# Latent attention with its exponentials and rotated halves in PSUM, and norms made on four token columns

## The chip, the cores and the metric

One core of a Trainium2 chip runs one program. The metric is the device time of one execution in microseconds (us). Engines are named as the profile names them: PE is TensorE (matrix products), PEld its weight loads, DVE VectorE, ACT ScalarE, POOL GpSimd, SP the engine that issues most of the DMAs. A core has 128 partitions; SBUF is the large on-chip memory, PSUM the one of eight banks of 512 fp32 columns into which PE writes.

## The reference

Four transformer layers over 512 tokens of 1024 features, fp32. The first two (windowed attention with sinks; block-sparse attention) end in an RMS norm, the "final norm". The last two modulate their input by a condition vector `c` and end in layer norms. The last one is latent attention, and it is the one that the change is mostly about:

```python
def mla_mixer(h, positions, w_in, q_norm_g, kv_norm_g, w_uq, w_uk, w_uv, w_out):
    proj = h @ w_in
    q_c, kv_c, k_r, z = jnp.split(proj, [MLA_Q_RANK, ...], axis=-1)   # 256, 128, 64, 2048 wide
    q_c, kv_c = rms_norm_2(q_c, q_norm_g), rms_norm_2(kv_c, kv_norm_g)
    q = jnp.einsum('bsr,rhd->bshd', q_c, w_uq)
    q_nope, q_rope = q[..., :MLA_NOPE], q[..., MLA_NOPE:]
    q_rope, k_rope = apply_rope(q_rope, ...), apply_rope(k_r, cos, sin)
    q_lat = jnp.einsum('bshd,rhd->bshr', q_nope, w_uk)
    ...
        s = jnp.einsum('bqhr,bkr->bhqk', ql, kv_c) + jnp.einsum('bqhd,bkd->bhqk', qr, k_rope)
        p = jax.nn.softmax(jnp.where(mask, s * ATTN_SCALE, -jnp.inf), axis=-1)
        o_lat = jnp.einsum('bhqk,bkr->bqhr', p, kv_c)
    ...
    o = jnp.einsum('bshr,rhd->bshd', o_lat, w_uv).reshape(B, S, MLA_WIDTH)
    return (o * jax.nn.silu(z)) @ w_out
# in the block around it
    x = layer_norm(DEEPNORM_ALPHA * x + (1.0 + gate[:, None, :]) * y, ln_g[l], ln_b[l])
```

## The kernel before

The kernel keeps activations transposed: features on the partitions, the 512 tokens along the columns. `hT` holds the residual stream as eight chunks of 128 features. Weights come in units of 128 x 1024. SP loads a unit into a ring of four (`raw`); ACT rounds it to its high part (`split_hi`, L531), POOL subtracts to get the low part (`split_lo`, L445), and PE makes every large product as three (`mm3`, L949 to L951: high by high, high by low, low by high). POOL does hardly anything else. Each engine has its own program, in the order in which it was written, and the engines wait for one another by semaphores that only count up.

**Norms.** A norm needs a sum over features, and features lie on partitions, so PE makes it: a product of the squares with `mean_w` (all entries 1/1024) puts the mean of each token, repeated on all 128 partitions, into a bank (`mean_square`, L979 for the final norm; L1335 for the latents). ACT takes the root of 128 x 512 values, DVE the reciprocal of 128 x 512 values (L1490, L1988, L1996), and the result, `rstd` or `rstd_q`, `rstd_kv`, multiplies the features. Behind the final norm DVE makes the modulated input (`modulate`, L1862 and L1857, with ACT's L766 between), for which PE waits with the next projection; then `residual` (L1871, eight instructions) and ACT's `residual_bias` (L773) turn `hT` into the residual term.

**Latents.** PE projects two query latents into banks 0 and 1, then the key/value latent into bank 2 and the rotary key into bank 3. In the fifth of the eight steps of each of the last two it makes the mean of the squares (banks 4 and 5). DVE multiplies the latents by gain and `rstd` (L1990, L1997) and makes the low parts (L1994); it rotates the key (L2002 to L2007). PE then makes the queries of the first two heads (`queries`), transposes the key/value latent (L1433), and goes on with `latent_queries`, which needs the low parts of the queries (`nope_lo`, L2012).

**Head loop.** Sixteen heads, in eight pairs. A pair has eight score blocks (m = 0 to 7; two heads by four blocks of 128 queries; block m has 128, 256, 384 or 512 keys), and two sets of buffers alternate. For a block PE makes the scores in a bank (`o_scores`, L1382 to L1385), DVE the maximum (L2028) and its scaled negative (L2030), ACT the exponential with its sum from the bank into SBUF tile `o_p` (L878), DVE the reciprocal of the sum (L2035) and the product `o_p` times it, in place (L2037), PE the transposes (`o_transpose`, L1393), ACT the copy into `o_pt` (L886), PE the latent output (`o_latent`, L1401). PE's order within a pair is: gate projection, scores 0 and 1, half of the second gate projection, and then for m = 2 to 10: transposes of m - 2, scores of m, latent output of m - 3, with quarters of the second gate projection at m = 5 and 9; then the next pair's queries, this pair's values, the next pair's latent queries. Meanwhile DVE rotates the next pair's queries (`rotate`, L2018, L2019, L2023), ACT and POOL split them (L863, L505). Ahead of the loop stand `residual(1)` on DVE and `residual_bias(1)` on ACT: the eight chunks of `hT` are multiplied by `rstd` and the gain column, then the bias is added. Only the sums behind the output projection need them.

## Time and profile before

| | us |
|---|---|
| median of 3 runs | 2105.71 (2102.74 to 2109.05) |
| the profiled execution, own time | 2105.03 |
| its span, first to last instruction | 2103.0 |
| PE busy | 1975.6 |
| DVE, ACT, POOL busy | 1016.6, 840.0, 805.9 |
| mean granted clock of PE | 0.971 |

The head loop runs from about 1690 to 1980 us of the span, the latents from 1644 to 1690, and the final norm at about 1280. The page's times are those of the profiled execution. A timeline row has the start, the duration (of several merged instructions, from the first start to the last end), the engine, the line and the operation with tiles and shape; in brackets the idle time of that engine before it and what ended it. In a row on groups, `x` is a count, followed by the busy time in us and the mean of one in ns. A granted clock of 1.00 is 2.4 GHz, one of 0.50 is 1.2 GHz; a value between them is a stretch in which it changed.

### The profile page before, as it was taken

What the parts mean: (1) busy time and instruction counts of PE and PEld (TensorE: products, weight loads), DVE (VectorE), ACT (ScalarE), POOL (GpSimd) and SP (SyncE); (2) the same over time, 40 slices, a digit from 0 to 9 for tenths busy, and PEclk for the clock granted to TensorE, in tenths of its full rate; (3) what the DMA queues carried; (4) which work ended last, traced back from release to release, by engine and by line L of the source; (5) the groups of instructions that cost most, each with busy time, mean ns of one, the idle gap of its engine ahead of it and who ended that gap; (6) DMA issues with size and microseconds to landing.
All of it is one profiled execution on the core that took longest, in us unless ns stands there. A gap on an engine that the chain in (4) does not pass through costs nothing.

```text
span 2103.0 us, 29110 instructions
## 1 busy us (share of the span) xinstructions
PE 1975.6 (94%) x9640; PEld 1638.0 (78%) x9640; DVE 1016.6 (48%) x2286; ACT 840.0 (40%) x1520; POOL 805.9 (38%) x382
## 2 busy tenths in 40 slices
PE   7999999999988999999999997999999789999896
PEld 5897888888777889878888886777887567777684
DVE  5555665211636666356553116658113655555414
ACT  4564222233444666342222325222222465555432
POOL 3533544444363100135444443445443332232340
PEclk9999999999999989999999999999999999999998
DMA  7532544222242112135442322323232111121121
GB/s 240 159 103 101 195 166 167 93 97 100 71 150 66 47 46 76 36 114 190 160 159 100 100 92 72 107 91 105 90 100 80 60 53 59 50 70 40 61 80 40
DMA packets 70026, 209.55 MB, mean 100 GB/s; under 512 B 9739, under 2 KB 15115, under 8 KB 69948
## 3 DMA queue, kind: packets, MB, share of 16 engines
q1 hardware_dynamic: 57724, 174.72, 25.2%
q10 hardware_dynamic: 12224, 33.85, 5.0%
q8 instruction: 41, 0.67, 0.1%
q14 instruction: 37, 0.30, 0.0%
HBM read 196.90 MB, written 8.49 MB: 98 GB/s over the span
## 4 chain that ended last, share of the span: by engine, by line
PE 58%; issue 21%; POOL 9%; DVE 8%; ACT 4%; POOLq 0%; DVEq 0%; ACTq 0%
PE bank L949 14%; PE bank L951 14%; PE bank L950 14%; POOL wsp L445 9%; PE bank L1227 3%; PE bank L1382 2%; DVE gen L2037 2%; PE bank L1200 1%; PE bank L1401 1%; PE bank L1211 1%; PE bank L1095 1%; PE bank L1393 1%; ACT wsp L531 1%; PE bank L1072 1%; PE bank L1223 1%
## 5 line engine op out<-in xcount | busy, mean ns | idle before, releaser
L445 POOL TENSOR_TENSOR wsp<-raw,wsp 128x1024 fp32r<-128x1024 f32 x294 | 730.5, 2491 | 1051.4 <-ACT wsp L531 1051.3
L949 PE MATMUL bank<-xs,wsp 128*128 128x512 f32 x1320 | 522.1, 396 | 19.5 <-issue 8.4
L950 PE MATMUL bank<-xs,wsp 128*128 128x512 f32 x1320 | 516.1, 391 | 0.0
L951 PE MATMUL bank<-xs,wsp 128*128 128x512 f32 x1320 | 516.1, 391 | 0.0
L531 ACT ACTIVATE wsp<-raw 128x1024 fp32r<-128x1024 f32 x294 | 306.9, 1052 | 229.9 <-PE bank L951 199.9
L949 PEld LDWEIGHTS bank<-xs,wsp 128*128 128x128 f32 x1320 | 249.4, 189 | 76.8 <-issue 15.3
L949 PE MATMUL bank<-xk,wsp 128*128 128x512 f32 x752 | 295.3, 393 | 9.4 <-DVE xk L1503 5.1
L950 PE MATMUL bank<-xk,wsp 128*128 128x512 f32 x752 | 294.2, 391 | 0.0
L951 PE MATMUL bank<-xk,wsp 128*128 128x512 f32 x752 | 294.2, 391 | 0.0
L951 PEld LDWEIGHTS bank<-xs,wsp 128*128 128x128 f32 x1320 | 249.2, 189 | 52.5
L950 PEld LDWEIGHTS bank<-xs,wsp 128*128 128x128 f32 x1320 | 249.6, 189 | 52.0 <-issue 1.4
L1503 DVE TENSOR_TENSOR xk<-mid,xk 128x512 fp32r<-128x512 f32 x86 | 61.1, 710 | 382.4 <-ACT xk L571 382.4
L571 ACT ACTIVATE xk<-mid 128x512 fp32r (+1 forms) x86 | 54.3, 631 | 331.2 <-PE bank L951 331.2
L949 PEld LDWEIGHTS bank<-xk,wsp 128*128 128x128 f32 x752 | 142.2, 189 | 41.6 <-DVE xk L1503 6.3
L951 PEld LDWEIGHTS bank<-xk,wsp 128*128 128x128 f32 x752 | 142.2, 189 | 29.8
L950 PEld LDWEIGHTS bank<-xk,wsp 128*128 128x128 f32 x752 | 142.3, 189 | 29.3
L1553 DVE CUSTOM_DVE_ANT_0 gen<-gen 128x1024 f32<-128x1024 f32 x48 | 124.7, 2598 | 14.0 <-issue 14.0
L587 ACT ACTIVATE tmp<-tmp 128x512 f32<-128x512 f32 x44 | 27.8, 632 | 245.4 <-DVE tmp L1541 245.4
L1543 DVE TENSOR_TENSOR mid<-bank,rstd 128x512 f32 (+1 forms) x44 | 30.4, 691 | 155.4 <-PE bank L951 155.4
L1227 PE MATMUL bank<-mid 128*128 128x64 f32 x640 | 90.1, 293 | 0.0
L734 ACT ACTIVATE mid<-mid,stat 128x128 f32<-128x128 f32 (+3 forms) x128 | 70.8, 554 | 38.6 <-DVE stat L1805 38.1
L1227 PEld LDWEIGHTS bank<-mid 128*128 128x128 f32 x640 | 84.7, 209 | 0.0
(286 smaller groups left out, 2504.2 us busy)
## 6 DMA issues: line engine op xcount, KB each, us to landing
raw<-weights SPq DMA_DIRECT2D x294, 512.0 KB, 3.5
gen<-ada ACTq DMA_DIRECT2D x48, 512.0 KB, 3.5
tmp<-mid SPq DMA_DIRECT2D x64, 128.0 KB, 3.0
bias_b<-bias_row ACTq DMA_DIRECT2D x1, 4096.0 KB, 38.1
mid<-bias_b SPq DMA_DIRECT2D x8, 512.0 KB, 3.9
hT<-xT SPq DMA_DIRECT2D x2, 1024.0 KB, 10.1
bias_a<-bias_row ACTq DMA_DIRECT2D x1, 2048.0 KB, 18.0
mid<-bias_a SPq DMA_DIRECT2D x8, 256.0 KB, 2.9
```

The costliest lines, as they stand in the source:

```text
L445: pool.tensor_tensor(wsp[:, slot, 1, :], raw[:, slot, :], wsp[:, slot, 0, :].bitcast(F32), ALU.subtract).then_inc(w_ready, 1)
L531: act.activation(wsp[:, u % RING, 0, :], raw[:, u % RING, :], ACT.Copy).then_inc(hi_done, 1)
L571: act.activation(xk[:, k % 2, 0, :], mid[:, i * RING + k, :], ACT.Copy).then_inc(xk_hi, 1)
L734: act.activation(b_s[b][:, r, 0:w], b_s[b][:, r, 0:w], ACT.Exp, scale=-1.0, bias=stat[:, b, r:r + 1], accum_out=stat[:, b, 4 + r:5 + r]).t ...
L949: pe.matmul(dst, w[0], x[0], start=first, stop=False)
L950: pe.matmul(dst, w[0], x[1], start=False, stop=False)
L951: return pe.matmul(dst, w[1], x[0], start=False, stop=last)
L1227: x = pe.matmul(dst[:, (1 + r) * HD:(2 + r) * HD], b_pt[b][:, r, kb * P:kb * P + P], vtok[:, r, kb * P + pp * HD:kb * P + pp * HD + HD], s ...
L1382: pe.matmul(dst[:, 0:w], ql[e][:, q], kvn[:, 0:w], start=True, stop=False)
L1503: dve.tensor_tensor(xk[:, k % 2, 1, :], mid[:, i * RING + k, :], xk[:, k % 2, 0, :].bitcast(F32), ALU.subtract).then_inc(xk_ready, 1)
L1553: dve.tensor_tensor_reduce(out=ada_st[k], in0=ada_st[k], in1=cond, scale=1.0, scalar=0.0, op0=ALU.mult, op1=ALU.add, accum_out=mod_sum[:, ...
L2037: dve.tensor_scalar(o_p[b][:, 0:w], o_p[b][:, 0:w], stat[:, b, 3:4], None, ALU.mult).then_inc(o_prob, 1)
```

## The change

In the head loop the exponential stays in the score bank, and DVE's product reads the bank and writes `o_p`. Since the bank is then read until the product is done, the scores of block m wait for the product of m - 2 (`o_prob`) and not for its exponential. ACT no longer waits for the transposes of m - 2; DVE's product does. The second rotation product is written into its own bank and the sums take one input from there; the rotated key is built in bank 7.

The residual of the last layer leaves DVE. POOL multiplies one chunk by `rstd` in each turn of its loop, behind the first weight split, and one behind the loop; ACT applies gain and bias to a chunk at the end of each pair.

In the final norm and at the latents PE writes the means of the four blocks of 128 tokens as four columns, one value for a token on its partition (`columns`); ACT and DVE work on 128 x 4 values, and PE spreads the result over the partitions again by four products with `ident` (`spread`), into the bank from which DVE reads it. The latents are multiplied by their gain before the norm is known; the normalised query latents stay in banks 0 and 1. The second half of the value projection waits until the residual has read bank 7.

```diff
+            def residual(j):
+
+                pool.tensor_tensor(hT[:, j, :], hT[:, j, :], rstd[:, :], ALU.mult).then_inc(mod_x, 1)
+
             with pool.Fori(0, PAIRS - 1) as hp:
                 for k in range(RING):
                     u = O_H + 5 + k
                     split_lo(u % RING, hp * RING + u)
+                    if k == 0:
+                        residual(hp)
                     if k == 2:
                         rope_lo(hp + 1)
+            residual(PAIRS - 1)
...
             def o_exp_of(m, r, hp):
 
                 b, w = m % 2, P * (m % 4 + 1)
-                if m >= 2:
-                    act.wait_ge(o_t, hp * 8 + (8 * r + m - 1))
+                scores = bank[SCORE_BANKS[r][b]][:, 0:w]
                 act.wait_ge(o_nm, hp * 8 + (8 * r + m + 1))
-                act.activation(o_p[b][:, 0:w], bank[SCORE_BANKS[r][b]][:, 0:w], ACT.Exp, scale=QK_SCALE,
-                               bias=stat[:, b, 1:2], accum_out=stat[:, b, 2:3]).then_inc(o_exp, 1)
+                act.activation(scores, scores, ACT.Exp, scale=QK_SCALE, bias=stat[:, b, 1:2],
+                               accum_out=stat[:, b, 2:3]).then_inc(o_exp, 1)
...
+                j = hp + r
+                act.wait_ge(mod_x, j + (16 + DC + 1))
+                act.activation(hT[:, j, :], hT[:, j, :], ACT.Identity, scale=modg[:, 1, bass.ds(j + 16, 1)],
+                               bias=modg[:, 1, bass.ds(j + 24, 1)]).then_inc(alpha_done, 1)
...
-            residual_bias(1)
...
+                if n == NORM_FINAL:
+                    act.activation(std_col[:, :], bank[7][:, 0:NB], ACT.Sqrt, bias=eps[:, 0:1]).then_inc(std_ready, 1)
+                    return
...
+            def columns(dst, src, first, last):
+
+                for blk in range(NB):
+                    x = pe.matmul(dst[:, blk:blk + 1], src[:, blk * P:blk * P + P], mean_w[:, 0:1],
+                                  start=first and blk == 0, stop=last and blk == NB - 1)
+                return x
+
+            def spread(dst, done, count):
+
+                pe.wait_ge(done, count)
+                for blk in range(NB):
+                    x = pe.matmul(dst[:, blk * P:blk * P + P], rstd_col[:, blk:blk + 1].to_broadcast([P, P]), ident[:, :],
+                                  start=True, stop=True)
+                return x
...
+                if n == NORM_FINAL:
+                    pe.wait_ge(sq_used, 8 * n + DC - 1)
+                    columns(bank[7], rstd, True, True).then_inc(sq_used, 1)
+                    spread(bank[7], rstd_ready, n + 1).then_inc(rstd_ready, 1)
+                    return
...
             for n in range(2):
+                if n:
+                    pe.wait_ge(mod_x, 2 * DC)
                 for q in range(4):
...
                 for k in range(DC):
-                    if k == 4:
+                    if k == 3:
                         pe.wait_ge(c_sq, 3 if n else 2)
                         for j in squared:
-                            x = pe.matmul(bank[at][:, :], mean_w[:, :], tmp[:, j, :], start=j == squared[0],
-                                          stop=j == squared[-1])
+                            x = columns(bank[at], tmp[:, j, :], j == squared[0], j == squared[-1])
                         x.then_inc(c_mean, 1)
+                    if k == 6:
+                        spread(bank[at], c_std, 5 if n else 2).then_inc(c_std, 1)
...
                 if m >= 2:
-                    pe.wait_ge(o_exp, hp * 8 + (8 * r + m - 1))
+                    pe.wait_ge(o_prob, hp * 8 + (8 * r + m - 1))
...
-                dve.tensor_tensor(tmp[:, 1, :], bank[3][:, :], sinb, ALU.mult).then_inc(r_part, 1)
+                dve.tensor_tensor(bank[3][:, :], bank[3][:, :], sinb, ALU.mult).then_inc(r_part, 1)
...
-                dve.tensor_scalar(o_p[b][:, 0:w], o_p[b][:, 0:w], stat[:, b, 3:4], None, ALU.mult).then_inc(o_prob, 1)
+                if m >= 2:
+                    dve.wait_ge(o_t, hp * 8 + (8 * r + m - 1))
+                dve.tensor_scalar(o_p[b][:, 0:w], bank[SCORE_BANKS[r][b]][:, 0:w], stat[:, b, 3:4], None, ALU.mult
+                                  ).then_inc(o_prob, 1)
...
             rotate(0, 0)
-            residual(1)
```

How the instructions stand on the engines is shown at three places, before and then with the change. An order row has the line, the operation, its tiles and shape, and the semaphores that it waits for.

VectorE in the head loop, the first block of a pair and the start of the second, before:

```order
L2028 TENSOR_REDUCE stat<-bank 128x1 [waits o_qk]
L2030 TENSOR_SCALAR stat<-stat 128x1 [waits o_max]
L2035 RECIPROCAL stat<-stat 128x1 [waits o_exp]
L2037 TENSOR_SCALAR gen<-gen,stat 128x128 [waits o_rec]
L2027 REGISTER_ALU
L2028 TENSOR_REDUCE stat<-bank 128x1 [waits o_qk]
L2030 TENSOR_SCALAR stat<-stat 128x1 [waits o_max]
```

and with the change:

```order
L2077 TENSOR_REDUCE stat<-bank 128x1 [waits o_qk]
L2079 TENSOR_SCALAR stat<-stat 128x1 [waits o_max]
L2084 RECIPROCAL stat<-stat 128x1 [waits o_exp]
L2088 TENSOR_SCALAR gen<-bank,stat 128x128 [waits o_rec]
L2076 REGISTER_ALU
L2077 TENSOR_REDUCE stat<-bank 128x1 [waits o_qk]
L2079 TENSOR_SCALAR stat<-stat 128x1 [waits o_max]
```

The order is the same; the product now takes its input from a bank, where it took it from `gen` (the tile `o_p`).

ScalarE from the end of one pair (splits of units for the next) into the first blocks of the next, before:

```order
L530 REGISTER_ALU [waits raw_in1]
L531 ACTIVATE wsp<-raw 128x1024 [waits unit_used]
L531 ACTIVATE wsp<-raw 128x1024 [waits unit_used,raw_in2]
L877 REGISTER_ALU
L878 ACT_TABLE_LOAD
L878 ACTIVATE gen,stat<-bank,stat 128x128 [waits o_nm]
L530 REGISTER_ALU [waits raw_in3]
L531 ACTIVATE wsp<-raw 128x1024 [waits unit_used]
```

and with the change:

```order
L538 REGISTER_ALU [waits raw_in1]
L539 ACTIVATE wsp<-raw 128x1024 [waits unit_used]
L930 REGISTER_ALU
L931 ISA [waits mod_x]
L931 ISA
L931 ACTIVATE hT<-hT,modg 128x512
L539 ACTIVATE wsp<-raw 128x1024 [waits unit_used,raw_in2]
L888 REGISTER_ALU
L889 ACT_TABLE_LOAD
L889 ACTIVATE bank,stat<-bank,stat 128x128 [waits o_nm]
L538 REGISTER_ALU [waits raw_in3]
L539 ACTIVATE wsp<-raw 128x1024 [waits unit_used]
```

The residual of one chunk has come between the two weight splits, ahead of the table load and the first exponential.

VectorE between the modulated input of the last layer and the first queries (`mid` and `gen` hold the latents, `gsp` the low parts), before:

```order
L1988 RECIPROCAL mid<-stdb 128x512 [waits c_std]
L1990 SCALAR_TENSOR_TENSOR mid<-bank,colp,mid 128x512 [waits vec_step]
L1990 SCALAR_TENSOR_TENSOR mid<-bank,colp,mid 128x512
L1994 TENSOR_TENSOR gsp<-mid,gsp 128x512 [waits qc_hi] x2
L1996 RECIPROCAL tmp<-mid 128x512 [waits c_std]
L1997 SCALAR_TENSOR_TENSOR gen<-bank,colp,tmp 128x512 [waits vec_step]
L2002 TENSOR_TENSOR tmp<-bank,gen 64x512 [waits unit_used,trig_ready]
L2003 TENSOR_TENSOR tmp<-bank,gen 64x512 [waits vec_step]
L2005 TENSOR_TENSOR tmp<-tmp 64x512 [waits kr_ready]
L2007 TENSOR_TENSOR gen_r<-tmp,gen_r 64x512 [waits kr_ready]
```

and with the change:

```order
L2031 TENSOR_SCALAR mid<-bank,colp 128x512 [waits c_sq]
L2031 TENSOR_SCALAR mid<-bank,colp 128x512 [waits vec_step]
L2033 RECIPROCAL rstd_col<-std_col 128x4 [waits c_std,vec_step]
L2036 TENSOR_TENSOR bank<-mid,bank 128x512 [waits c_std]
L2036 TENSOR_TENSOR bank<-mid,bank 128x512
L2039 TENSOR_TENSOR gsp<-bank,gsp 128x512 [waits qc_hi] x2
L2042 TENSOR_SCALAR gen<-bank,colp 128x512 [waits c_sq]
L2044 RECIPROCAL rstd_col<-std_col 128x4 [waits c_std,vec_step]
L2046 TENSOR_TENSOR gen<-gen,bank 128x512 [waits c_std]
L2051 TENSOR_TENSOR tmp<-bank,gen 64x512 [waits unit_used,trig_ready]
L2052 TENSOR_TENSOR bank<-bank,gen 64x512 [waits vec_step]
L2054 TENSOR_TENSOR bank<-tmp,bank 64x512 [waits kr_ready]
```

The gain products stand ahead of the reciprocals, these have 4 columns where they had 512, and the products with the spread norm (`bank` as second input) follow them.

## Rows read from the trace of the kernel before

**Rows 1.** The page: busy time of each engine.

```profile
PE 1975.6 (94%) x9640; PEld 1638.0 (78%) x9640; DVE 1016.6 (48%) x2286; ACT 840.0 (40%) x1520; POOL 805.9 (38%) x382
```

**Rows 2.** Waits of PE in the head loop: total us, times, longest.

```profile
PE bank L1393 <- DVE gen L2037: 22.7, 11, 5.7
```

**Rows 3.** Timeline of PE in one pair: start, us, instruction, idle time before.

```profile
1729.39 0.38 PE L1382 MATMUL bank<-gen 128*128 128x128 f32 x2
...
1735.72 0.33 PE L1393 MATMUL bank<-ident,gen 128*128 128x128 f32 x1 [2.31 <-DVE gen L2037]
...
1753.43 0.47 PE L949 MATMUL bank<-gsp,wsp 128*128 128x512 f32 x1
```

**Rows 4.** Windows of PE: length, busy (instructions), clock, DMA share, GB/s.

```profile
1736.50:1737.00 0.50, 0.50 (x3) 0.69 0.50 98
...
1740.00:1740.50 0.50, 0.50 (x4) 0.90 0.00 0
```

**Rows 5.** Timeline of DVE in the same pair.

```profile
1731.27 4.39 DVE L2037 TENSOR_SCALAR gen<-gen,stat 128x128 f32<-128x128 f32 x1
...
1737.29 0.55 DVE L2028 TENSOR_REDUCE stat<-bank 128x1 f32<-128x384 f32 x1
...
1738.77 0.16 DVE L2035 RECIPROCAL stat<-stat 128x1 f32<-128x1 f32 x1 [0.74 <-ACT gen L878]
1738.97 0.42 DVE L2037 TENSOR_SCALAR gen<-gen,stat 128x384 f32<-128x384 f32 x1
```

**Rows 6.** Timeline of POOL there.

```profile
1728.57 7.01 POOL L445 TENSOR_TENSOR wsp<-raw,wsp 128x1024 fp32r<-128x1024 f32 x3
```

**Rows 7.** Timeline of ACT there, and a group of ACT lines: xcount, busy us, mean ns.

```profile
1730.58 0.37 ACT L878 ACTIVATE gen<-bank,stat 128x128 f32<-128x128 f32 x1
...
L773 ACT ACTIVATE hT<-hT,modg 128x512 f32<-128x512 f32 x4 | 2.7, 723 | 0.0
```

**Rows 8.** Timelines of DVE and POOL in the first pair.

```profile
1697.01 0.41 DVE L2028 TENSOR_REDUCE stat<-bank 128x1 f32<-128x256 f32 x1
...
1698.44 1.02 DVE L2037 TENSOR_SCALAR gen<-gen,stat 128x256 f32<-128x256 f32 x1
...
1694.66 4.65 POOL L445 TENSOR_TENSOR wsp<-raw,wsp 128x1024 fp32r<-128x1024 f32 x2 [7.06 <-ACT wsp L531]
```

**Rows 9.** Groups of DVE lines, forms apart: xcount, busy us, mean ns.

```profile
L1827 DVE TENSOR_SCALAR gen<-bank,stat 128x64 f32<-128x64 f32 x64 | 18.1, 283 | 45.1 <-PE bank L1227 33.9 <-PE bank L1238 10.6
...
L2037 DVE TENSOR_SCALAR gen<-gen,stat 128x512 f32<-128x512 f32 x16 | 7.8, 487 | 0.6
...
L1946 DVE TENSOR_SCALAR mid<-bank,colp 128x512 f32<-128x512 f32 x8 | 6.1, 805 | 9.3 <-PE bank L951 9.3
```

**Rows 10.** Timelines of PE and DVE at the first pair.

```profile
1697.14 0.47 PE L1393 MATMUL bank<-ident,gen 128*128 128x128 f32 x1 [5.74 <-DVE gen L2037]
...
1683.96 7.50 DVE L1871 SCALAR_TENSOR_TENSOR hT<-hT,modg,rstd 128x512 f32<-128x512 f32 x8
```

**Rows 11.** Timelines of PE and DVE at the latents.

```profile
1659.47 1.88 PE L1335 MATMUL bank<-tmp,mean_w 128*128 128x512 f32 x4
...
1680.46 0.47 PE L949 MATMUL bank<-gsp,wsp 128*128 128x512 f32 x1 [3.57 <-DVE gsp L2012]
...
1669.23 3.34 DVE L1996 RECIPROCAL tmp<-mid 128x512 f32<-128x512 f32 x1
```

**Rows 12.** Timelines of PE and DVE at the final norm.

```profile
1289.89 0.76 PE L949 MATMUL bank<-wsp,xs 128*128 128x512 f32 x1 [6.58 <-DVE xs L1857]
...
1284.07 3.35 DVE L1490 RECIPROCAL rstd<-stdb 128x512 f32<-128x512 f32 x1 [2.23 <-ACT stdb L558]
```

**Rows 13.** Timeline of PE in the second attention: products with few columns.

```profile
652.24 1.00 PE L1168 MATMUL bank<-gen 128*128 128x14 f32 x8
```

**Rows 14.** Windows of PE in the second attention, columns as in rows 4.

```profile
722.00:723.00 1.00, 0.19 (x2) 1.00 0.71 217
...
744.00:745.00 1.00, 1.00 (x7) 0.50 0.00 0
```

## What I expect of the time

> **What bounds the kernel now.** I read the page first, then the waits of TensorE in the head loop, then one pair of heads on every engine, then the two stretches in which norms are made. The page says that TensorE is busy for 94% of the span [rows 1]. So an edit counts only where TensorE stands still, or where it runs at its lower clock because it stood still. In the head loop almost all its standing still has one cause: it waits for VectorE's normalised probabilities, L2037: 22.7 us, of which the first pair has 5.74, seven pairs 2.31 each, and three short waits the rest [rows 2, 3, 10]. One of the seven shows the pattern: the scores of the first block start at 1729.39, TensorE does what it can, stands for 2.31 us, and goes on at 1735.72 with the first transpose [rows 3]. Behind that gap the granted clock falls to the lower level (1.2 GHz) at 1736.7 and is back at 2.4 GHz at 1740.1: the half microseconds in which it changes show 0.69 and 0.90 [rows 4]. Why is VectorE late? Its multiplication of 128 columns took 4.39 us [rows 5], though it started at 1731.27, early enough. GpSimd was in three weight splits back to back, from 1728.57 to 1735.58 [rows 6], and VectorE's instruction ended at 1735.66, 0.08 us after the last of them. That is the cause I take. The same rows hold the control: in the first pair, while GpSimd worked from 1694.66 to 1699.31, VectorE's maximum over 256 columns of PSUM took 0.41, but its multiplication of 256 columns, from SBUF to SBUF, took 1.02 [rows 8], where even 512 columns take 0.487 on average over the loop [rows 9]. So the SBUF-to-SBUF multiplication is held by GpSimd, and the instruction that reads PSUM isn't.
>
> **The pair of heads, parts removed.** With the exponentials left in PSUM the multiplication reads PSUM, and by the control it isn't held. The 2.31 us of standing go. With them goes the lower clock: 3.4 us, in which half the work is done, so 1.7 us. Together 4.0 us of the 24.0 that lie between 1729.39 and 1753.43 [rows 3, 4].
>
> **The pair of heads, parts added.** First, the multiplication is slower in itself. From SBUF, 512 columns took 0.487 [rows 9]. From PSUM, with one column as scalar, 64 columns took 0.283, and 512 columns with two such scalars 0.805 [rows 9]; that leaves about 1.04 ns for a column, so 0.75 for 512, 0.62 for 384, 0.48 for 256 and 0.35 for 128, which is 0.27 to 0.07 more than before, 0.67 for four blocks. Second, ScalarE gets a residual instruction of 0.72 to 0.8 us (the one with columns as scalars stands in [rows 7]) at the end of a pair, directly ahead of the next pair's first exponential, and ScalarE is tight there: that exponential began at 1730.58, and its row names no idle time before it. It moves to about 1731.4. Maximum to finished product then ends near 1732.5, and TensorE asks for it at 1733.4: 0.8 us of slack, so it is hidden. Third, the later blocks. From a block's maximum to its product there pass 2.1 us before (1737.29 to 1739.39 for 384 columns, [rows 5]) and 2.3 with the slower product. For the third block TensorE has only some 1.8 us of other work meanwhile, since the second block's product is now also late: a wait of 0.5 to 0.75. For the fourth, seventh and eighth blocks VectorE's own chain of maximum and product runs behind by 0.1, 0.3 and 0.45. That makes 1.5, of which about 0.3 was there before among short gaps: I take 1.2 net, with 0 (the chain catches up) and 2.4 (each of eight blocks waits 0.3) as bounds. The transposes already stood ahead of the scores in TensorE's order, so that scores now wait for the product and not for the exponential adds no wait. Nor does ScalarE's dropped wait give anything. A pair gains 4.0 - 1.2 = 2.8, and seven pairs 19.6.
>
> **The first pair.** The residual (eight instructions on VectorE, 7.50 us, [rows 10]) no longer stands ahead of the first maximum, so the 5.74 us of standing [rows 10] go, and the lower clock behind them costs at least the same 1.7. Less 1.2 that is 6.3. GpSimd does the residual's product in its loop now: half of a weight split of 2.34 us [rows 6], 1.2 us a pair. Behind it on GpSimd stand the splits of units that are first needed a pair later, so 20 us of slack hide it, and without that cover it would cost 1.2 a pair. ScalarE's wait for it comes 30 us later. The residual of all chunks is needed only by the output projection's sums after the loop.
>
> **Latents.** From 1659.47, where the mean square starts, to 1680.46, where the first latent queries start after 3.57 us of standing [rows 11], there pass 21.0 us. TensorE's own work there is 14.0 without the means (60 products of 0.226 us, the pace of the stretches that do not wait, and four transposes). VectorE's 3.35 us reciprocals [rows 11, 12] and its multiplication and sums held by GpSimd made the standing. They shrink to four columns, or take one input from PSUM; counted forward, the low halves of the queries are ready just as TensorE has finished the kvn transposes, so the 3.57 go. But TensorE's means cost more: three full products (six instructions, 2.6 us, four of them at 0.43 each in the first, [rows 11]) become twelve one-column products and eight spreading ones. Each is two instructions, and instructions with 14 columns came 0.11 apart [rows 13], no cheaper than with 128, since a weight load goes with each. 40 x 0.11 = 4.4. So 14.0 + 4.4 + 0.2 of start-up = 18.6, a gain of 2.4. Bounds: 0.5 (a wait of 2 is left) and 3.6.
>
> **Final norm.** TensorE stood for 6.58 us [rows 12] behind a chain in which the reciprocal has 3.35 [rows 12]. It becomes one of four columns, 0.2 (128 x 1 took 0.16, [rows 5]), and the root loses 0.35 (0.72 against 0.37 for 512 and 128 columns, [rows 7]). That is 3.5 less. The spread adds eight instructions at 0.11, 0.9, or 1.8 at the lower clock: 2.2 of gain, bounds 1.2 and 3. The new wait of the second half of the value projection, for bank 7, finds the residual long done.
>
> **The sum** against the profiled execution's own time, 2105.03 (span 2103.0; the median of the three runs is 2105.71): 19.6 + 6.3 + 2.4 + 2.2 = 30.5, so 2074.5.
>
> **The rivals.**
> 1. *The clock still falls in every pair.* The new short waits sit in the stretch of small products, and these might not hold the clock. The gain of 1.7 is lost eight times: 2074.5 + 13.6 = 2088. Against it: in the attention before, a microsecond with a busy share of only 0.19 left the clock at its upper level [rows 14]. 0.13.
> 2. *The waits in the pair vanish.* If ScalarE's exponential gets shorter when it writes PSUM, the chain of 2.3 us shrinks to TensorE's 1.8. Then 8 x 1.2 = 9.6 more: 2065. No row has ScalarE writing to PSUM. The Trainium skill, page "PSUM — Partial Sum Buffer", section "Specifications (TRN2)", says that ScalarE writes PSUM faster than SBUF; no run here shows it. 0.12.
> 3. *ScalarE becomes the bound at a pair's start.* If the residual with its offsets from registers takes 1.6 instead of 0.8, the slack is gone, and up to 0.8 comes in each pair: 2081. 0.06.
> 4. *The change doesn't do what it says:* VectorE is held whatever it reads while GpSimd works. Then the 19.6 and most of the 2.4 stay away, and 6.3 + 2.2 are left: 2097. Against it stands the control in [rows 8]. The Trainium skill, page "SBUF — State Buffer", section "Who interferes with whom", has the rule: GpSimd shares a pair of ports with VectorE, held for a whole instruction, and only a VectorE instruction in a two-port mode or with two SBUF inputs needs it. By that rule, the trace agrees: 0.41 against 1.02. 0.03.
> 5. *Slower: the lower clock stays through the small products.* In the attention before, a stretch ran at half clock while TensorE was fully busy, with 7 instructions in a microsecond [rows 14] against 9 at 0.11 apart. If a wait early in a pair starts such a stretch and it lasts through the 14 us of small products, each pair loses 3 (7 against 9) to 7 (half); with 5 that is 8 x 5 = 40: 2114. It decides from 3.8 us of loss in a pair. 0.04.
>
> **How the numbers follow.** My forecast has 0.62; with its bounds it spans 2067 to 2082. The range 2062 to 2089 takes in rivals 1 to 3 and leaves out 4, 5 and the tails, some 0.1 to 0.15. What can be told from no change is 0.3%, 6.3 us. Faster by more: all but rival 5 and a sliver, 0.95; within: 0.01; slower: 0.04.
>
> **What would show it.** In the pairs: no wait of TensorE for the first product over 0.3 us, a clock of 1.00 throughout, and a multiplication of 128 columns at 0.35 beside GpSimd's splits; and 21.2 us from the first scores to the end of the first head pair's products, where 24.0 stood. At the latents: TensorE's wait for the low halves under 0.5, forty instructions on one-column and spreading products. At the final norm: some 4.4 us of standing in all in place of 6.58. I am wrong if products from PSUM are still stretched while GpSimd works, if a half-clock stretch is left in each pair, or if ScalarE's first exponential starts later than 2.8 us after the first scores.

## The result, and the profile after

The changed kernel takes 2069.03 us (median of 4 runs, 2067.32 to 2070.8) against 2105.3 of the kernel before: a ratio of 0.983 (95% interval 0.981 to 0.984), 36.3 us less where I had forecast 30.5 less. The profiled execution took 2069.23 us, its span is 2067.4 (2103.0 before), so the two traces differ by 35.6.

The page of the changed kernel, busy time of each engine, beside [rows 1]:

```profile
PE 1963.5 (95%) x9688; PEld 1637.3 (79%) x9688; DVE 969.7 (47%) x2281; ACT 839.3 (41%) x1520; POOL 813.4 (39%) x390
```

PE has 48 instructions more and is all the same busy 12 us less: the time that it no longer spends at its lower clock outweighs them. The waits of PE between 1683 and 1955 us, beside [rows 2] (line waited at, what for, total us, times, longest):

```profile
PE bank L1430 <- DVE gen L2088: 8.0, 16, 0.7
PE bank L963 <- DVE xk L2093: 2.5, 1, 2.5
```

22.7 us have become 8.0, in sixteen pieces, two in each pair. The third pair in the timeline of PE, beside [rows 3]: its first scores, its first, third and last transposes:

```profile
1752.55 0.38 PE L1419 MATMUL bank<-gen 128*128 128x128 f32 x2
...
1756.42 0.27 PE L1430 MATMUL bank<-ident,gen 128*128 128x128 f32 x1
...
1760.09 0.55 PE L1430 MATMUL bank<-ident,gen 128*128 128x128 f32 x3 [0.63 <-DVE gen L2088]
...
1771.00 0.66 PE L1430 MATMUL bank<-ident,gen 128*128 128x128 f32 x4 [0.36 <-DVE gen L2088]
```

The first transpose no longer waits; the third block's does, for 0.63, and the eighth's, for 0.36. From one pair's first scores to the next there pass 34.5 us, each of the seven times, where 42.0 passed in the first pair and 37.6 to 37.8 in the others. Why the first transpose doesn't wait is in the timelines of DVE, POOL and ACT at the same place, beside [rows 5 to 7]:

```profile
1755.12 0.35 DVE L2088 TENSOR_SCALAR gen<-bank,stat 128x128 f32<-128x128 f32 x1
...
1759.42 0.62 DVE L2088 TENSOR_SCALAR gen<-bank,stat 128x384 f32<-128x384 f32 x1
```

```profile
1754.62 2.39 POOL L446 TENSOR_TENSOR wsp<-raw,wsp 128x1024 fp32r<-128x1024 f32 x1 [0.55 <-ACT wsp L539]
1756.97 1.28 POOL L515 TENSOR_TENSOR hT<-hT,rstd 128x512 f32 x1
```

```profile
1751.37 0.80 ACT L931 ACTIVATE hT<-hT,modg  x1
...
1754.45 0.32 ACT L889 ACTIVATE bank<-bank,stat 128x128 f32<-128x128 f32 x1
```

The product of 128 columns takes 0.35 us in the middle of a weight split (4.39 before). ACT's residual of 0.80 stands ahead of the first exponential, which starts 1.90 us after the first scores (1.19 before, [rows 3, 7]); the product is done at 1755.47 and PE asks for it at 1756.42. The clock holds through the wait that is left, in half a microsecond without any work (windows of PE: length, busy time and instructions, clock, DMA share, GB/s), beside [rows 4]:

```profile
1759.50:1760.00 0.50, 0.00 (x0) 1.00 0.82 336
1760.00:1760.50 0.50, 0.41 (x4) 1.00 0.09 33
```

The groups by line with shapes apart (count, busy us, mean ns; then idle time before), beside [rows 9]:

```profile
L2088 DVE TENSOR_SCALAR gen<-bank,stat 128x512 f32<-128x512 f32 x16 | 12.0, 751 | 0.6
L2088 DVE TENSOR_SCALAR gen<-bank,stat 128x128 f32<-128x128 f32 x16 | 5.6, 351 | 0.8 <-DVE stat L2084 0.3
L889 ACT ACTIVATE bank<-bank,stat 128x128 f32<-128x128 f32 x16 | 5.4, 340 | 9.3 <-DVE stat L2079 9.3
```

At the final norm, PE (beside [rows 12]): four columns of means, four spreading products, the first value product.

```profile
1280.51 1.02 PE L990 MATMUL bank<-mean_w,rstd 128*128 128x1 f32 x8 [2.27 <-DVE rstd L1510]
1282.10 2.07 PE L998 MATMUL bank<-ident,rstd_col 128*128 128x128 f32 x8 [0.57 <-DVE rstd_col L1528]
...
1286.64 0.77 PE L963 MATMUL bank<-wsp,xs 128*128 128x512 f32 x1 [2.47 <-DVE xs L1898]
```

From the means to the first value product there pass 6.1 us where 7.9 passed. At the latents (beside [rows 11]) nothing waits any more between the means and the latent queries:

```profile
1657.03 1.84 PE L990 MATMUL bank<-mean_w,tmp 128*128 128x1 f32 x16
...
1660.91 1.05 PE L998 MATMUL bank<-ident,rstd_col 128*128 128x128 f32 x8
...
1676.33 0.48 PE L963 MATMUL bank<-gsp,wsp 128*128 128x512 f32 x1
```

**Where the 35.6 us come from.** I laid the two traces of PE beside one another by instructions that stand in both, and read how far the changed kernel is ahead:

| stretch | ahead at its end | gained in it |
|---|---|---|
| start to the final norm (the change leaves it alone) | 1.5 | 1.5 |
| final norm, until the clock is back | 2.5 | 1.0 |
| rest of the third layer (not touched) | 2.2 | -0.2 |
| latent projections to the first scores | 3.8 | 1.6 |
| head loop | 33.3 | 29.5 |
| output projection (not touched) | 35.6 | 2.3 |

The head loop's 29.5 splits into standing and clock. Standing: 22.7 - 8.0 = 14.7. Clock: before, PE was at work at the lower clock for 5.4 us in the first pair, 3.2 in the second and 3.4 in each of six more, 29.1 in all, of which half is lost: 14.5. After, the loop has no such stretch. 14.7 + 14.5 = 29.2.

### The profile page after: what moved, and what is told of

The parts are those of the page before. It is cut to its first block, busy times and chain, and to the rows that moved or that the text cites. A ratio compares the mean times of both kernels' runs of the same rounds, so it can differ in the third digit from the quotient of the medians.

```text
span 2067.4 us, 29274 instructions
## 1 busy us (share of the span) xinstructions
PE 1963.5 (95%) x9688; PEld 1637.3 (79%) x9688; DVE 969.7 (47%) x2281; ACT 839.3 (41%) x1520; POOL 813.4 (39%) x390
## 4 chain that ended last, share of the span: by engine, by line
PE 62%; issue 21%; POOL 9%; DVE 6%; ACT 2%; POOLq 0%; DVEq 0%; ACTq 0%
PE bank L963 16%; PE bank L965 15%; PE bank L964 15%; POOL wsp L446 9%; PE bank L1261 3%; PE bank L1234 1%; PE bank L1245 1%; PE bank L1419 1%; PE bank L1129 1%; PE bank L1438 1%; PE bank L1017 1%; PE bank L1106 1%; PE bank L1257 1%; PE bank L1430 1%; PE bank L1117 1%
## 5 line engine op out<-in xcount | busy, mean ns | idle before, releaser
L965 PEld LDWEIGHTS bank<-xk,wsp 128*128 128x128 f32 x752 | 141.7, 188 | 29.5
```

Of the source, the lines that this page charges most:

```text
L965: return pe.matmul(dst, w[1], x[0], start=False, stop=last)
```

## The experiments

All ran on the same chips as runs of the kernel before, whose median was 2103.8 to 2105.5 us.

| run | what it is | median us | ratio to before (95%) |
|---|---|---|---|
| e1_exp_psum | before, exponentials in PSUM | 2076.35 | 0.987 (0.985 to 0.988) |
| e2_pool_late | before, GpSimd's splits held back | 2078.14 | 0.988 (0.986 to 0.989) |
| e3_residual | before, residual moved | 2106.75 | 1.001 (1.000 to 1.002) |
| e4_exp_sbuf | changed, exponentials back in SBUF | 2101.29 | 0.998 (0.998 to 0.999) |
| e5_norms | before, norms on columns | 2101.29 | 0.998 (0.997 to 0.999) |
| e6_forms | changed, one VectorE instruction more a pair | 2080.35 (one run) | |
| v1_late_sbuf | changed, SBUF and splits held back | 2065.21 | 0.981 (0.980 to 0.982) |
| v2_gate | changed, gate projection cut otherwise | 2067.1 | 0.982 (0.980 to 0.983) |
| v3_filler | changed, fillers at the final norm | 2066.48 | 0.981 (0.980 to 0.983) |
| v4_all | v1, v2 and v3 together | 2060.97 | 0.979 (0.978 to 0.981) |
| r_after | changed, again | 2068.4 | 0.983 (0.982 to 0.984) |

### Is it the exponentials' place? (e1_exp_psum)

```diff
-                if m >= 2:
-                    act.wait_ge(o_t, hp * 8 + (8 * r + m - 1))
+                scores = bank[SCORE_BANKS[r][b]][:, 0:w]
                 act.wait_ge(o_nm, hp * 8 + (8 * r + m + 1))
-                act.activation(o_p[b][:, 0:w], bank[SCORE_BANKS[r][b]][:, 0:w], ACT.Exp, scale=QK_SCALE,
-                               bias=stat[:, b, 1:2], accum_out=stat[:, b, 2:3]).then_inc(o_exp, 1)
+                act.activation(scores, scores, ACT.Exp, scale=QK_SCALE, bias=stat[:, b, 1:2],
+                               accum_out=stat[:, b, 2:3]).then_inc(o_exp, 1)
...
-                    pe.wait_ge(o_exp, hp * 8 + (8 * r + m - 1))
+                    pe.wait_ge(o_prob, hp * 8 + (8 * r + m - 1))
...
-                dve.tensor_scalar(o_p[b][:, 0:w], o_p[b][:, 0:w], stat[:, b, 3:4], None, ALU.mult).then_inc(o_prob, 1)
+                if m >= 2:
+                    dve.wait_ge(o_t, hp * 8 + (8 * r + m - 1))
+                dve.tensor_scalar(o_p[b][:, 0:w], bank[SCORE_BANKS[r][b]][:, 0:w], stat[:, b, 3:4], None, ALU.mult
+                                  ).then_inc(o_prob, 1)
```

> The kernel before, with one part of the change alone: exponentials stay in the score bank, VectorE's product reads the bank. My theory (VectorE's SBUF-to-SBUF product is held while GpSimd works, its product from PSUM isn't; the standing drags the clock down): pairs 2 to 8 take 34.5 us each in place of 37.7, so 22 us less. In the first pair the residual still stands ahead on VectorE: the wait of 5.74 us shrinks to about 2, so 4 less, and the clock there is uncertain by 2.7. Sum: about 2079 us (2075 to 2082). Rival, the gain comes from the residual that moved or from the norms: within 5 us of 2105.

Measured 2076.35: this part alone gains 28.3 us, where the whole change gains 36.3. Pairs take 34.5 us. In the first pair the wait is 1.66 (timeline of PE), and no lower clock follows it, nor is there one anywhere in this run's loop: the first pair takes 36.7.

```profile
1694.14 0.33 PE L1392 MATMUL bank<-ident,gen 128*128 128x128 f32 x1 [1.66 <-DVE gen L2038]
```

The pairs have the length of the changed kernel's, so the residual that the change puts on ScalarE and GpSimd costs them nothing. Ahead of the loop, though, this trace has a half-clock stretch that neither the kernel before nor the changed one has, from 1677.5 to 1684.3 (window of PE):

```profile
1680.00:1680.50 0.50, 0.50 (x3) 0.50 0.00 0
```

PE is at work for 5.2 us of it, so some 2.6 are lost. It starts in the standing for the latent queries, which the kernel before has at the same length (3.57 us, [rows 11]) without a fall. On the other hand the clock stays up at the output projection, where it fell before, which gives 2.3. The two nearly cancel: from the first scores of the loop to the output projection this trace gains 27.4 us, where the changed kernel gains 29.5.

### Is GpSimd the cause? (e2_pool_late)

```diff
                     u = O_H + 5 + k
+                    if k == 0:
+                        pool.wait_ge(o_prob, hp * 8 + 8)
                     split_lo(u % RING, hp * RING + u)
```

> The kernel before, exponentials still in SBUF; one wait is added: in each turn of its loop GpSimd begins its first weight split only when the eighth product of the pair is done, so that no split runs beside the products. My theory (GpSimd holds the product of 128 columns): no product over 0.5 us, TensorE's wait of 2.31 us and the half-clock stretch behind it are gone although nothing moves to PSUM; a pair takes 33.5 to 34.0 us, 7 x 3.9 = 27 less, and 4 less in the first pair: about 2074 us (2070 to 2079). Rival, the source in PSUM matters by itself or the scheduling of ScalarE does: no gain, 2105 us, and slower (over 2110) if TensorE now waits for the late splits.

Measured 2078.14, and pairs of 34.0 us. GpSimd splits one unit ahead of the products, stands until the eighth product is done, and then splits two (timelines of POOL and DVE, second pair, whose first scores start at 1724.83):

```profile
1724.00 2.37 POOL L445 TENSOR_TENSOR wsp<-raw,wsp 128x1024 fp32r<-128x1024 f32 x1
1742.92 4.72 POOL L445 TENSOR_TENSOR wsp<-raw,wsp 128x1024 fp32r<-128x1024 f32 x2 [16.54 <-DVE gen L2039]
```

```profile
1726.71 0.29 DVE L2039 TENSOR_SCALAR gen<-gen,stat 128x128 f32<-128x128 f32 x1
```

The same instruction, SBUF to SBUF, takes 0.29 where it took 4.39 [rows 5]. In the second to seventh pairs the wait and the lower clock are gone without anything in PSUM; the first keeps 1.60 us of waiting (1.66 in e1). The last pair, for which I hadn't placed a wait, still has its 2.31 us and a half-clock stretch behind it. That settles the cause, and it shows a second remedy whose pairs are 0.5 us shorter than the change's. The total is no lower than e1's all the same: the last pair keeps its wait, and the clock falls at the output projection, where it didn't in e1.

### The residual alone (e3_residual)

```diff
+                    if k == 0:
+                        residual(hp)
...
-            residual_bias(1)
...
-            residual(1)
```

> The kernel before, with one part alone: the residual goes to GpSimd's loop and to the end of ScalarE's pair. By my theory this is a loss by itself: GpSimd's product of 1.28 us stands in the run of splits that holds VectorE's first product, so the hold, TensorE's wait and the pair grow by 1.3 us, from 37.7 to 39.0, seven times 9 us more; in the first pair the wait of 5.74 becomes 2.31 + 1.3 = 3.6, 2 less. Sum: about 2112 us (2106 to 2114). Rival, the residual costs nothing wherever it stands and the first pair gains 5.74 and its clock: 2098 us.

Measured 2106.75, 2 us slower than before: the sign is right and the size isn't. The profiled execution is the fastest of the ten (2101.05; the slowest took 2108.79), so its trace shows the pattern but not the 2 us; what differs in the slower ones wasn't profiled. In five of seven later pairs the first product is held to the end of a run of splits that is now longer (DVE and POOL, second pair), and PE waits 3.5 us:

```profile
1723.83 4.91 DVE L2047 TENSOR_SCALAR gen<-gen,stat 128x128 f32<-128x128 f32 x1
```

```profile
1720.42 4.72 POOL L445 TENSOR_TENSOR wsp<-raw,wsp 128x1024 fp32r<-128x1024 f32 x2
1725.11 1.25 POOL L514 TENSOR_TENSOR hT<-hT,rstd 128x512 f32 x1
1726.33 2.33 POOL L445 TENSOR_TENSOR wsp<-raw,wsp 128x1024 fp32r<-128x1024 f32 x1
```

In the two others (the third and the fifth pair) GpSimd had paused for 0.54 us right before the split in which VectorE's product arrives, and the hold broke up: 1.98 us at the first product and 2.24 at the second (third pair):

```profile
1762.62 1.98 DVE L2047 TENSOR_SCALAR gen<-gen,stat 128x128 f32<-128x128 f32 x1
...
1765.96 2.24 DVE L2047 TENSOR_SCALAR gen<-gen,stat 128x256 f32<-128x256 f32 x1
```

I had counted one pattern for all. And the first pair gave 6.2 where I expected 2: there the first product took 1.60 us, and GpSimd had paused for 1.10 before the split. The kernel before has the same in its first pair, behind a pause of 7.06 [rows 8] (DVE):

```profile
1695.16 1.93 DVE L2037 TENSOR_SCALAR gen<-gen,stat 128x128 f32<-128x128 f32 x1
```

It ended at 1697.09, between the two splits of the run, the first of which ended at 1697.01. In the traces of all the runs the SBUF-to-SBUF instructions of 128 columns that met GpSimd in the loop fall into two groups. Eight came in the first instruction of a run, behind a pause of at least 0.53 us (one in the kernel before, one in e5, three each in e3 and e4), and ended 0.1 us after that instruction. 27 came in a later instruction of a run (the kernel before, e2 to e6) and ended 0.1 to 0.15 us after the last. What stays open is why.

### The exponentials taken back (e4_exp_sbuf)

The first diff of this section, turned round, on the changed kernel.

> The changed kernel with its exponentials back in SBUF, all else as changed. My theory: VectorE's first product is held again, and 1.3 us longer than in the kernel before, for GpSimd's residual product lies in the run of splits: pairs of 39.0 us in place of 34.5, 8 x 4.5 = 36 more, about 2104 us (2098 to 2108). Rival, the hold costs what it did before (3.2 a pair): 2095. Rival, the exponentials' place isn't what gained: under 2080.

Measured 2101.29, 32 us more than the changed kernel; pairs of 38.0 to 40.0 us, but the first 35.0. The two kinds of hold are those of the run before. So without the exponentials in PSUM all else that the change does is worth 3.4 us against the runs beside it (2104.68).

### The norms alone (e5_norms)

The changed kernel's norms, columns and rotation on the kernel before, with the exponentials and the residual as they were.

> The kernel before with the column norms (final norm and latents) and the rotation in PSUM alone; exponentials in SBUF, residual on VectorE ahead of the loop. From the two stretches of the changed kernel I now read 1.0 us at the final norm, where part of the standing removed lay in a half-clock stretch that stays, and 2.1 at the latents: about 2101.5 us (2099 to 2104), and pairs of 37.7 us as before. Rival, the terms as forecast, 2.2 and 2.4: 2100. Rival, the norms carry the 5 us by which the changed kernel beat my forecast: 2096.

Measured 2101.29: 4.2 us less than before, nearest to the 2101.5 of my new reading; 2100 can't be told from it, 2096 can. Pairs take 37.6 as before, the first 41.2, 0.8 less.

### Which instructions are held (e6_forms)

```diff
+                if not tail and r == 0:
+                    dve.tensor_scalar(s, a, 2.0, None, ALU.mult)
+                elif not tail:
+                    dve.tensor_tensor(d, a, s, ALU.mult)
+                elif r == 0:
+                    dve.tensor_tensor(d, a, c, ALU.mult)
+                else:
+                    dve.tensor_scalar(d, a, 2.0, None, ALU.mult)
```

(`a`, `c` and `d` are 128 columns of an SBUF tile that is free there, `s` 128 columns of the score bank.)

> The changed kernel with one VectorE instruction more in each pair, ahead of the first product, while GpSimd is in a weight split; 128 columns, its output used by nothing. In pairs 1, 3, 5 a product by a constant from SBUF to the score bank; in pairs 2, 4, 6 a product of an SBUF tile and the bank, to SBUF; in pair 7 a product of two SBUF tiles, to SBUF; in pair 8 a product by a constant from SBUF to SBUF. If what GpSimd holds is the form with all its data in SBUF, the first two take about 0.3 to 0.4 us and the last two end with GpSimd's run, several us. Rival, the output's place doesn't matter and an SBUF input is enough: the first is held too. Rival, only the form with one SBUF input and one SBUF output (pair 8) is held: pair 7 takes 0.35.

The groups of DVE lines with shapes apart:

```profile
L2089 DVE TENSOR_TENSOR stdb<-stdb 128x128 f32<-128x128 f32 x1 | 5.1, 5141 | 0.0
L2091 DVE TENSOR_SCALAR stdb<-stdb 128x128 f32<-128x128 f32 x1 | 5.1, 5066 | 0.0
L2085 DVE TENSOR_SCALAR bank<-stdb 128x128 f32<-128x128 f32 x3 | 0.8, 274 | 0.0
L2087 DVE TENSOR_TENSOR stdb<-stdb,bank 128x128 f32<-128x128 f32 x3 | 0.8, 268 | 0.0
```

Four forms with 128 columns, at the same place of a pair, each begun inside a GpSimd instruction: 5.1 us where all data lie in SBUF, 0.27 where one operand, be it the output, lies in PSUM. One bank in the instruction is enough. The pairs with the two short forms still take 34.5 us; in the pair with the first long one PE waits 3.9 us.

All data in SBUF isn't enough for a hold, though. The instructions on one column lie in SBUF too (`stat` to `stat`), and they are never held; eight and nine of them began and ended inside an instruction of GpSimd in the kernel before and took no longer than the others (its groups of DVE lines in the head loop):

```profile
L2030 DVE TENSOR_SCALAR stat<-stat 128x1 f32<-128x1 f32 x64 | 9.8, 154 | 2.2
L2035 DVE RECIPROCAL stat<-stat 128x1 f32<-128x1 f32 x64 | 10.5, 164 | 47.8 <-ACT gen L878 47.8
```

From how many columns on a product is held, no run shows. The Trainium skill, page "SBUF — State Buffer", section "Who interferes with whom", says that VectorE contends with GpSimd in a two-port mode or with two SBUF inputs, and that the loser is then blocked for the whole of the other's instruction. The trace agrees for two SBUF inputs (5.14) and for one SBUF input beside a bank (0.27); that the form with one SBUF input and SBUF output (5.07) ran in such a mode, the trace doesn't show. And the page speaks of one instruction of GpSimd, where here the hold went on over three of them, 5.1 us in all.

### The remedy that keeps SBUF (v1_late_sbuf)

The changed kernel with e4's edit, and e2's wait ahead of the split of k = 0, and once more behind the loop:

```diff
             residual(PAIRS - 1)
+            pool.wait_ge(o_prob, 8 * PAIRS)
```

> The changed kernel with exponentials back in SBUF and GpSimd's splits held until the eighth product of each pair (the last pair too). If the hold by GpSimd is the whole cause and the product from SBUF is 0.07 to 0.27 us shorter, pairs take 34.0 us in place of 34.5: 8 x 0.45 = 3.6 less than the changed kernel, about 2065.5 us (2063 to 2069). Rival, the later splits make TensorE or ScalarE wait at a pair's end: over 2071.

Measured 2065.21. Pairs of 34.0 us. PE's waits for the products in the loop:

```profile
PE bank L1434 <- DVE gen L2090: 4.3, 10, 0.6
```

GpSimd's idle time in a pair pays for it; VectorE's product is the cheaper one from SBUF (0.35 for 256 columns, 0.48 from PSUM). The median is 3.2 to 3.8 us below the changed kernel's two medians, with intervals that overlap; the 0.5 us of each pair are read from the traces.

### The waits that are left (v2_gate)

```diff
-                project(u0 + 1, z[1][:, :], hp, part=range(4))
+                project(u0 + 1, z[1][:, :], hp, part=range(3))
                 for m in range(2, 11):
+                    if m == 4:
+                        project(u0 + 1, z[1][:, :], hp, part=range(3, 4))
```

> The changed kernel with TensorE's second gate projection cut otherwise: three of its eight steps ahead of the first transposes where four stood, and the fourth ahead of the third block's transposes, where 0.63 us of waiting is left in each pair. If that wait and the 0.35 later come from VectorE's chain of maximum and product, the chain now starts 0.4 us earlier and the fourth step fills the rest: about 0.5 us less in each pair, 2065 us (2063 to 2068). Rival, the wait only moves to the second or fourth block: 2069.

Measured 2067.1, no more than 2 us below the changed kernel's two medians, with intervals that overlap; the traces show it: pairs of 34.23 us, 0.25 less, half of what I expected. The 0.63 before the third block's transposes has become 0.36 before the second's, and the 0.35 before the eighth's has stayed:

```profile
PE bank L1430 <- DVE gen L2090: 5.4, 15, 0.4
```

So the wait partly moved, as the rival had it; the last one doesn't come from the chain's early start.

### The clock at the final norm (v3_filler)

```diff
+                    filler(6)
                     pe.wait_ge(sq_used, 8 * n + DC - 1)
                     columns(bank[7], rstd, True, True).then_inc(sq_used, 1)
+                    filler(2)
                     spread(bank[7], rstd_ready, n + 1).then_inc(rstd_ready, 1)
+                    filler(10)
```

(`filler(n)` makes n products of `ident` and `mean_w` into bank 0, which nothing reads.)

> The changed kernel with 18 small products more on TensorE, of no use but to keep it at work, in its three gaps at the final norm (6, 2 and 10, about 0.22 us each). If the half-clock stretch there comes from the standing, it goes: the spread, the wait and the first value products run at full clock, 3 to 3.5 us less: 2066 us. Rival, the clock falls all the same: the fillers then take 0.43 us each, the last ten 4.3 us in a gap of 2.5, and it is 2 to 3 us slower: 2071.5.

Measured 2066.48, 2 to 2.5 us less than the changed kernel's two medians; the intervals overlap, so the stretch itself must show it. In the changed kernel the clock falls at 1281.5 and is back at 1291.7, and 7.2 us of PE's work lie in between (windows of PE):

```profile
1281.50:1282.00 0.50, 0.03 (x1) 0.50 0.00 0
...
1291.50:1292.00 0.50, 0.50 (x3) 0.78 0.00 0
```

With the fillers it never falls there; the spread takes 1.16 in place of 2.07 (window and timeline of PE):

```profile
1282.00:1282.50 0.50, 0.50 (x7) 1.00 0.00 0
```

```profile
1283.27 1.16 PE L998 MATMUL bank<-ident,rstd_col 128*128 128x128 f32 x8
1284.27 2.40 PE L1009 MATMUL bank<-mean_w,ident 128*128 128x128 f32 x20
1286.90 0.47 PE L963 MATMUL bank<-wsp,xs 128*128 128x512 f32 x1 [0.24 <-DVE xs L1904]
```

v4, which has the same fillers, has no fall there either, and the eleven traces without fillers all have one, so this is not chance: the standing is the cause of the lower clock here, and work without use prevents it. By the traces it saves 1.0 us before the first value product (7.4 us after the last product of the layer ahead, where 8.4 passed) and 2.5 behind it, half of the 5.1 us that ran at the lower clock there.

### All together (v4_all)

The edits of v1, v2 and v3 in one kernel.

> All that paid, in one kernel: exponentials in SBUF with GpSimd's splits held back, the other cut of the second gate projection, and the small products at the final norm. If the parts add: 2065.2 less 2.5 for the fillers and 1 to 2 for the gate projection (0.43 us of waiting are left in a pair): about 2061.5 us (2059 to 2064). Rival, they overlap or the clock gives it back elsewhere: 2064 to 2067.

Measured 2060.97, the fastest here, 0.979 of the kernel before (0.978 to 0.981), 7.4 to 8.1 us below the changed kernel's two medians. The parts add up. PE's waits for the products in the loop:

```profile
PE bank L1440 <- DVE gen L2098: 1.7, 9, 0.3
```

Pairs take 33.8 us.

### The changed kernel again (r_after)

> The changed kernel again, beside the two others. Median 2069.0 as before (2067 to 2071). The pairs take 34.5 us each again. Whether the half-clock stretches behind the value projection's wait (1.2 us, at 1358) and at the output projection's start (2.5 us of standing) come is not fixed by the program by my theory: one of them may be there now, 1.7 to 2.7 us each. Rival, the change removed them for good: none of them in this run either.

Measured 2068.4; pairs of 34.5. Neither of the two half-clock stretches came, so this run goes with the rival. The other traces say more. Behind the value projection the clock fell in all four kernels with the old final norm (before, e1, e2, e3), and of the nine traces with the new one only in v3. In turn, ahead of the last layer (at 1626 us in the changed kernel) it fell in eight of those nine, all but v3, and in none with the old norm. So it goes with the form of the norm: the new one moved a half-clock stretch from one place to another, 1.4 us gained and 1.6 lost. My theory that chance puts it there was wrong for this place. Why v3 goes with the old ones, and v4, which has the same fillers, with the new, stays open. At the start of the output projection, which is the same in all and where PE stands for 2.5 us and again for 1.5, it fell in e2, e3, e4, e5, e6, v2, v4 and the kernel before, and stayed up in e1, v1, v3 and both runs of the changed kernel; no part of the change goes with that. A window of PE there, first of the kernel before, then of the changed one:

```profile
1983.00:1983.50 0.50, 0.50 (x3) 0.50 0.00 0
```

```profile
1949.50:1950.00 0.50, 0.50 (x4) 1.00 0.00 0
```

The same standing is followed by a fall in one kernel and not in the next. So it is with the 3.6 us of standing at the old form of the latents: the clock fell in e1 and e2 and stayed up in e3 and the kernel before. What decides it the runs don't show, so the 2.3 us gained there aren't safely the change's.

## Why the prediction was right, and where it was off

- **What bounds, and why VectorE is late: right.** e1 and e4 show that the place of the exponentials carries 28 to 32 us; e2 takes GpSimd away and has the effect with nothing moved; e6 shows the form that is held, in four variants. The control in [rows 8] was weaker than I took it to be: it set a maximum that reads PSUM beside a multiplication in SBUF, two things that differ. Only e1 and e6 part the place from the operation.
- **Parts removed in a pair, 4.0 us: right.** In each of the seven pairs behind the first, the standing of 2.31 and the 1.7 of lower clock went: no stretch at half clock is left in any of the eight pairs, which rival 1 (2088) would have had. Rivals 4 (held anyway) and 5 (half clock through the small products) fell with it.
- **Parts added in a pair, 1.2 net: somewhat too much.** The product's own cost was right to the hundredth (0.351, 0.484, 0.618, 0.751 us for 128 to 512 columns, against 0.35, 0.48, 0.62, 0.75 worked out). The third block waits 0.63 (0.5 to 0.75 forecast) and the eighth 0.35 (0.45), but those that I gave the fourth and seventh, 0.4 together, aren't there. Part of the reason is that ScalarE's exponential is shorter into PSUM, 0.340 against 0.365 on average for 128 columns (one of them in [rows 7]) and 0.662 against 0.688 for 512, 0.025 each: rival 2 in kind, but not enough to remove the waits. A pair gained 3.1 to 3.2 where I had 2.8: 22.0 for seven against 19.6.
- **ScalarE's slack at a pair's start: right.** The residual took 0.80; the product was ready 0.95 us before PE asked (0.8 forecast). GpSimd's residual took 1.28 (1.2) and delayed nobody. What I hadn't seen is that this part, made alone, is a loss (e3): it is free only because the products no longer mind GpSimd.
- **The first pair, 6.3: too small, 7.5.** I took 1.7 for the clock as "at least"; by the windows of before, PE was at work for 5.4 us at the lower clock there, 2.7 lost. 5.74 + 2.7 - 1.0 of new waits is 7.4.
- **Latents, 2.4: right in mechanism and nearly in size.** From the first latent projection to the latent queries 34.7 us pass where 36.6 passed, and in the changed kernel 1.0 us more of that work fell at the lower clock, 0.5 lost: 1.9 + 0.5 = 2.4. 0.3 was given back before the first scores, so 1.6 is what arrived.
- **Final norm, 2.2: wrong in size, 1.0.** The standing shrank by 3.5, as worked out (2.27 + 6.58 to 2.27 + 0.57 + 2.47), and the spread cost 2.1 at the lower clock (the forecast had 0.9, or 1.8 at the lower clock, and took 1.3). The step that failed is that I priced the remaining standing removed at its full length. The clock had already fallen, and it came back 5.1 us after the first value product (3.1 before): the earlier start was spent on work at half speed. A gain that falls into a half-clock stretch counts about half. v3 shows the rest: with the clock kept up, about 2.5 us more arrive. The sign that I named, 4.4 us of standing, was also at odds with my own term: 6.58 less 3.5 is 3.1, and 3.04 came (0.57 + 2.47).
- **What I didn't forecast:** 2.3 us at the output projection, where the clock fell before and didn't after, and 1.3 net ahead of the final norm and behind it. Of the latter, the part ahead of the norm is run-to-run: in eleven traces with the same program up to the final norm, its means start anywhere from 1278.7 to 1282.0 us.

So the 5.1 us between forecast and trace are 3.5 in stretches that the change leaves alone, and 3.6 more in the loop (2.4 in seven pairs, 1.2 in the first), less 2.0 at the norms. The 3.5 are luck as far as the runs show, and without them the forecast is off by 1.6.

## What to carry to other kernels

When a VectorE instruction is long for its size, look at what GpSimd does in the same microseconds: a multiplication of 128 columns or more with all its data in SBUF can be held over a whole run of GpSimd's, and either one operand in PSUM or another time for GpSimd's work frees it; the second costs nothing on VectorE, and here it was the better one, by 0.5 us a pair. Count a wait that disappears together with the lower clock behind it, but price a start that moves earlier inside a half-clock stretch at half. Where PE must stand for several microseconds and the next work is dense, a few idle products can be worth more than the norm made cheaper.

## What the runs showed of the hardware that I had not expected

- The hold reaches over several instructions of GpSimd: 5.14 and 5.07 us for 128 columns, over three instructions and to within 0.2 us of the end of the run, where two variants with an operand in PSUM took 0.27. But a product that came in the first instruction of a run, behind a pause of 0.53 us or more, got in after that one, eight times of eight (0.8 to 2.0 us).
- The hold doesn't reach instructions on one column: SBUF to SBUF in the midst of a split, they took 0.15 and 0.16 us, as elsewhere.
- The output in PSUM frees an instruction as well as an input does (0.274 us).
- 18 small products of no use kept the clock at 1.00 over a stretch where it had been at 0.50 for 10.2 us, in v3 and again in v4.
- The same standing of 2.5 and 1.5 us at the output projection lowered the clock in eight traces and not in five; and a norm that came 3.5 us of standing shorter moved a half-clock stretch from 1361 us to 1626 us, in code that is the same (eight of nine traces).
- A wait of 0.63 us amid small products did not lower the clock in any of the eight pairs.
